# Function tables loaded ahead of use by one-column activations, and two norms that share one set of squares

## The reference

```python
h = h + _mixer(_rmsnorm(h, norm_mix_w), w_in, ...)      # retention and latent attention, gated
h = h + _swiglu(_rmsnorm(h, norm_ffn_w), ...)           # silu(u @ w_gate) * (u @ w_up) @ w_down
h = _rmsnorm(h, norm_final_w)[:, N_META:]               # end of block 1
...
for layer in range(2):                                  # block 2
    h = _rmsnorm_2(x, mix_norm_g[layer])                # layer 0: the second norm in a row
    x = x + (_even_mixer(h, ...) if layer == 0 else _odd_mixer(h, ...))
    x = x + square(relu(_rmsnorm_2(x, mlp_norm_g[layer]) @ w1)) @ w2

def _rmsnorm(xf, w):
    return xf * lax.rsqrt(jnp.mean(xf * xf, axis=-1, keepdims=True) + 1e-6) * w
```

## Time and profile before

| what | value |
|---|---|
| median of three runs | 1150.87 us (1149.94 to 1151.02) |
| the profiled execution, its time | 1150.63 us |
| span of its trace | 1148.5 us |
| PE busy | 1107.4 us (96%) |
| DVE busy | 732.2 us (64%) |
| ACT busy | 516.2 us (45%) |
| mean granted clock of PE | 0.982 of full |
| DMA | 177.64 MB, 155 GB/s |
| the chain that ended last | PE 79%, DVE 11%, ACT 6%, issue 2%, DMA 2% |

### The profile page before, as it was taken

One profiled execution on the slowest core, in us unless ns is written; L12 is line 12 of the kernel. 1 busy time (PEld: TensorE's weight loads), 2 busy tenths in 40 slices (PEclk: granted clock), 3 DMA queues, 4 the chain that ended last, 5 costly groups with the idle time before them and its releaser, 6 DMA issues.

```text
span 1148.5 us, 21011 instructions
## 1 busy us (share of the span) xinstructions
PE 1107.4 (96%) x8656; PEld 1058.8 (92%) x8656; DVE 732.2 (64%) x790; ACT 516.2 (45%) x521; POOL 2.2 (0%) x5
## 2 busy tenths in 40 slices
PE   8999999999999999989989999999988999999998
PEld 7998887899899999978879999999988999999998
DVE  5754646668666766667745665555589776655553
ACT  5523426444544444473755434342543464433431
POOL 0000000000000000000000000000000000000000
PEclk8999999999999999998989999999989999999999
DMA  9683242346456566726234455555244334655531
GB/s 307 188 219 111 74 129 74 111 148 189 140 153 202 169 197 181 235 94 220 74 111 147 146 191 175 194 171 170 88 144 145 116 114 146 216 184 183 182 110 37
DMA packets 162589, 177.64 MB, mean 155 GB/s; under 512 B 4800, under 2 KB 148288, under 8 KB 162536
## 3 DMA queue, kind: packets, MB, share of 16 engines
q1 hardware_dynamic: 160704, 174.58, 48.1%
q10 hardware_dynamic: 1832, 2.30, 1.1%
HBM read 175.29 MB, written 1.57 MB: 154 GB/s over the span
## 4 chain that ended last, share of the span: by engine, by line
PE 79%; DVE 11%; ACT 6%; issue 2%; DMA 2%; ACTq 0%; SPq 0%; DVEq 0%
PE proj L440 48%; PE aux L846 21%; DVE wlo L1525 4%; DVE f L1528 2%; DVE f L1525 2%; ACT whi L1108 2%; PE aux L497 1%; DMA gamma_rows<-f 1%; PE aux L608 1%; PE aux L597 1%; DVE f L1531 1%; ACT u L1308 1%; DMA f<-in_x_dram 1%; PE aux L720 1%; PE aux L705 0%
## 5 line engine op out<-in xcount | busy, mean ns | idle before, releaser
L440 PE MATMUL proj<-u,whi 128*128 128x256 f32 (+1 forms) x2912 | 537.8, 286 | 10.2 <-DVE wlo L1525 4.1
L440 PEld LDWEIGHTS proj<-u,whi 128*128 128x128 f32 x2912 | 455.6, 191 | 18.2 <-issue 7.4
L1525 DVE TENSOR_TENSOR wlo<-raw,whi 128x2048 fp32r<-128x2048 f32 (+2 forms) x179 | 374.7, 2093 | 149.1 <-ACT whi L1108 141.3
L440 PE MATMUL proj<-u,wlo 128*128 128x256 f32 (+1 forms) x1456 | 413.5, 284 | 0.0
L1108 ACT ACTIVATE whi<-raw 128x2048 fp32r<-128x2048 f32 (+2 forms) x173 | 309.5, 1789 | 105.4 <-PE aux L846 38.3
L440 PEld LDWEIGHTS proj<-u,wlo 128*128 128x128 f32 x1456 | 278.8, 191 | 0.0
L846 PE MATMUL aux<-v,whi 128*128 128x256 f32 x1376 | 249.9, 283 | 2.7 <-DVE v L1525 2.5
L846 PEld LDWEIGHTS aux<-v,whi 128*128 128x128 f32 x1376 | 214.1, 192 | 3.4 <-issue 3.4
L846 PE MATMUL aux<-v,wlo 128*128 128x256 f32 x688 | 194.6, 283 | 0.0
L846 PEld LDWEIGHTS aux<-v,wlo 128*128 128x128 f32 x688 | 131.8, 192 | 0.0
L440 PE MATMUL proj<-v,whi 128*128 128x256 f32 (+1 forms) x564 | 103.8, 286 | 1.8 <-DVE v L1528 1.2
(11 more groups left out here) (291 smaller groups left out, 750.9 us busy)
## 6 DMA issues: line engine op xcount, KB each, us to landing
raw<-in_mlp_w_dram SPq DMA_DIRECT2D x64, 1024.0 KB, 5.3
raw<-in_w_in_dram SPq DMA_DIRECT2D x21, 1024.0 KB, 6.8
raw<-in_od_w_in_dram SPq DMA_DIRECT2D x12, 1024.0 KB, 5.4
raw<-in_w_ffn_gate_dram SPq DMA_DIRECT2D x22, 512.0 KB, 4.0
raw<-in_w_ffn_up_dram SPq DMA_DIRECT2D x22, 512.0 KB, 5.2
raw<-in_w_ffn_down_dram SPq DMA_DIRECT2D x21, 512.0 KB, 5.3
raw<-in_ev_w_in_dram SPq DMA_DIRECT2D x10, 1024.0 KB, 5.3
raw<-in_w_ret_out_dram SPq DMA_DIRECT2D x4, 1024.0 KB, 5.3
```

Of the source, the lines that this page charges most:

```text
L440: ins = mm(o, w_of(a, k), x_of(b, k), start=first and k == 0 and j == 0, stop=last and k == kt - 1 and j == 2, skip_group_check=skip)
L1525: return ve.tensor_tensor(o, a, b, op)
```

## The change

There are two parts.

**Tables.** `table_for(func)` is an ACTIVATE of one column into a scratch column. The compiler puts the table load in front of it, and not in front of the next real use. It stands at some twenty places of ACT's program. One gelu (`za1`) is moved ahead of the second half's Exps. Both programs hold 25 ACT_TABLE_LOADs in all (the loops hold none).

**Norms.** With s = mean(x^2), the combined factor is 1/sqrt(mean(x^2 (g^2 + eps)) + eps^2), since mean((x g)^2)/(s + eps) + eps, times (s + eps), is just that sum. The weights of the sum of squares become g^2 + eps, broadcast (`gains_and_eps`), and one root gives the factor. The first norm's own sum is now a separate set of eight products of ones (`first_sums`) between `sq0` and `sq1`; its root and reciprocal, and the scaling of x, come later.

```diff
@@ PE
+    weights = gains_and_eps[:, k:k + 1].to_broadcast([P, P]) if second else C("ones")
+    ins = mm(aux[:, 0, 0:tokens], weights, sq_of(tokens)[:, k, :], start=k == 0, stop=k == KT - 1, ...)
-                if second and c:
-                    for k in range(0 if c == 1 else 2 * c, 2 * c + 2):
-                        ins = mm(aux[:, 1, 0:S], C("ones"), f("f3", 0, KT, S)[:, k, :], ...)
...
+            def first_sums():
+                for k in range(KT):
+                    ins = mm(aux[:, 1, 0:S], C("ones"), sq_of(S)[:, k, :], start=k == 0, stop=k == KT - 1)
+                ins.then_inc(sems["first_sums"], 1)
...
             project("sq0", t0=META, t=S, gate=by_pair(2, second=True))
-            for name in ("sq1", "sk0", "sk1"):
+            first_sums()
+            project("sq1", t0=META, t=S)
+            turn_norm(2)
+            for name in ("sk0", "sk1"):
                 project(name, t0=META, t=S)
-            turn_norm(2)
@@ ACT
+            def table_for(func):
+                A.run(act(small[:, 17:18], one, func))
...
             eng.wait_ge(sems["small_ready"], 1)
+            table_for(ACT.Sqrt)
...
+                        if c == 3:                       # norm("wo"), norm("eo"), norm("oo")
+                            table_for(ACT.Sqrt)
...
-                    if second:
-                        A.run(ins)
-                        for k in (2 * c, 2 * c + 1):
-                            ins = act(f("f3", 0, KT, S)[:, k, :], x2[:, k, :], ACT.Square, scale=V("final", k))
...
             norm("wo", lambda k: V("ffn", k), 1)
+            pump(loop_first["ffn"])
+            table_for(ACT.Tanh)
             hidden_layer(FFN)
-            norm(0, lambda k: both_gains[:, k:k + 1], 2, second=True)
-            eng.wait_ge(sems["second_mean"], 1)
-            A.post(act(r_all[:, 2, 0:S], r_all[:, 2, 0:S], ACT.Sqrt, bias=eps, scale=1.0 / D), "second_root")
+            table_for(ACT.Sqrt)
+            norm(0, lambda k: both_gains[:, k:k + 1], 2, eps_ap=eps_sq)
+            eng.wait_ge(sems["first_sums"], 1)
+            root(aux[:, 1, 0:S], r_all[:, 1, 0:S], 1.0 / D, eps, "first_root")
             for j, name in enumerate(("sq", "sk")):
                 pump(index[f"{name}0"])
...
             A.post(act(stat[:, 4:6], stat[:, 2:4], ACT.Sqrt, bias=eps, scale=1.0 / 512), "vg_root")
+            table_for(ACT.Exp)
             sb_exp_abs(0)
             sb_exp_abs(1)
             sb_log(0)
             sb_log(1)
+            table_for(ACT.Exp)
             pump(index["za1"])
             sb_attn(0)
             sb_attn(1)
             pump(index["sv0"])
+            table_for(ACT.Gelu_apprx_tanh)
+            read_out("za1")
+            A.post(act(za[:, :, 0:512], za[:, :, 0:512], ACT.Gelu_apprx_tanh), "gelu_ready")
+            table_for(ACT.Exp)
             sb_exp_abs(2)
             sb_exp_abs(3)
             sb_log(2)
             sb_log(3)
-            read_out("za1")
-            A.post(act(za[:, :, 0:512], za[:, :, 0:512], ACT.Gelu_apprx_tanh), "gelu_ready")
+            table_for(ACT.Exp)
             pump(index["sv1"])
...
             pump(index["gates"])
+            table_for(ACT.Exp)
...
             A.post(act(ab, ab, ACT.Ln, bias=one), "gates_log")
+            table_for(ACT.Tanh)
@@ DVE
-            eng.wait_ge(sems["root_ready"], 5)
-            B.run(ve.reciprocal(rf, rms))
-            B.run(tt(rm, rf, rf, ALU.mult))
-            B.post(tt(rm, rm, aux[:, 1, 0:S], ALU.mult), "second_mean")
-            eng.wait_ge(sems["second_root"], 1)
-            B.run(ve.reciprocal(rm, rm))
-            B.post(tt(rms, rf, rm, ALU.mult), "rms_ready")
+            norm_scale(2)
...
+            qk_raw(0, 0, urgent=True)
+            eng.wait_ge(sems["late_in"], 16)
+            B.run(ve.tensor_copy(f("f5", 0, 16, 64)[0:16], ...))
+            B.run(ve.tensor_copy(ident_r, C("ident")))
+            B.run(ts(mask_r, LC("mask_strict")[:, 0:P], 1.0, ALU.subtract, MASKED, ALU.mult))
+            qk_raw(0, 1)
+            eng.wait_ge(sems["first_root"], 1)
+            B.run(ve.reciprocal(rf, rf))
+            final_scale(0, 2)
+            qk_raw(1, 0)
+            token_factors(1)
+            final_scale(2, 6)
+            qk_raw(1, 1)
```

More of the change, by code:

```diff
@@ L280, in build @@
         both_gains = small[:, 64:72]
+        gains_and_eps, eps_sq = small[:, 8:16], small[:, 3:4]
         x_tok = f("f1", 0, 3, D)
@@ L1295, in _, with norm @@
             pump(index["mo1"])
-            def norm(source, gain, norm_no, second=False):
+            def norm(source, gain, norm_no, eps_ap=eps):
                 for c in range(4):
                     if isinstance(source, str):
+                        if c == 3:
+                            table_for(ACT.Sqrt)
                         pump(index[f"{source}{min(c + 1, 3)}"])
@@ L1321, in norm @@
                 eng.wait_ge(sems["sumsq"], norm_no + 1)
-                root(aux[:, 0, 0:S], r_all[:, 0, 0:S], 1.0 / D, eps, "root_ready")
+                root(aux[:, 0, 0:S], r_all[:, 0, 0:S], 1.0 / D, eps_ap, "root_ready")
             def hidden_layer(d):
@@ L1565, in _ @@
             B.run(ve.memset(eps, EPS))
+            B.run(ve.memset(eps_sq, EPS * EPS))
             B.run(ve.memset(gn_eps, GN_EPS))
@@ L1609, in _ @@
                      par[:, PAR_COLS["mix2"][0]:PAR_COLS["mix2"][0] + KT], ALU.mult))
+            final_gains = par[:, PAR_COLS["final"][0]:PAR_COLS["final"][0] + KT]
+            B.run(tt(gains_and_eps, final_gains, final_gains, ALU.mult))
+            B.run(ts(gains_and_eps, gains_and_eps, EPS, ALU.add))
             pump(index["rq0"] - AHEAD + 2)
@@ L1961, in _, with qk_raw, final_scale @@
             B.run(ts(qg8, V("sb_q"), 0.125, ALU.mult))
-            for j, name in enumerate(("sq", "sk")):
-                for c in range(2):
-                    b = arrive(f"{name}{c}", urgent=j == c == 0)
-                    freed(tt(pre[j][:, 2 * c:2 * c + 2, :], proj[:, b:b + 2, 0:S], bc(rms, 2), ALU.mult))
-                    if j == 0:
-                        for k in range(4 * c, 4 * c + 4):
-                            B.run(stt(x2[:, k, :], x2[:, k, :], V("final", k), rf, ALU.mult, ALU.mult))
+            def qk_raw(j, c, urgent=False):
+                b = arrive(f"{'sq' if j == 0 else 'sk'}{c}", urgent=urgent)
+                freed(tt(pre[j][:, 2 * c:2 * c + 2, :], proj[:, b:b + 2, 0:S], bc(rms, 2), ALU.mult))
+            def final_scale(k0, k1):
+                for k in range(k0, k1):
+                    B.run(stt(x2[:, k, :], x2[:, k, :], V("final", k), rf, ALU.mult, ALU.mult))
+            qk_raw(0, 0, urgent=True)
+            eng.wait_ge(sems["late_in"], 16)
+            B.run(ve.tensor_copy(f("f5", 0, 16, 64)[0:16], C("ident")[0:16, 0:16][:, :, None].to_broadcast([16, 16, 64])))
+            B.run(ve.tensor_copy(ident_r, C("ident")))
[8 more added lines that the diff above has]
+            qk_raw(1, 1)
             def per_token(name, dst, width=256):
```

15 lines of the change are left out of this document (4 added, 11 removed).

## The result

The changed kernel takes 1139.52 us in the median of its first four runs (1136.87 to 1140.48), the one before 1150.94. The ratio is 0.9898, with a 95% interval of 0.9884 to 0.9911, so 1.0% less. The forecast was 1138.3, in a range of 1134 to 1143. In a second group of six runs the same kernel took 1138.06 (1134.75 to 1141.11; 0.9895 of before, 0.9878 to 0.9913). The kernel before took 1149.1 to 1154.1 in all groups.

A forecast was written before the change was run, and what follows sets the result against it. PE was taken as the bound, busy 1107.4 of 1148.5 us, leaving only its gaps to win. The terms -1.3 - 1.5 - 1.0 - 0.5 + 0.2 - 8.3 = -12.4 took 1150.63 to 1138.2; forecast 1138.3, range 1134 to 1143.

The forecast's parts named there:

- The second norm, -8.3: Second norm: without PE's wait for a low half and the slower clock behind it, `za2` starts 8.3 us earlier.
- Rival A: Second norm: PE waits for the first sums instead, and the clock may fall again; 1139.3 to 1142 us, chance 0.12.
- the stated bound: Second norm: if PE never waits from 494.69 on, its 0.54 us wait goes too, giving -8.8.
- Start, -1.3: Start of the kernel: the Sqrt load moves to the very start, and 1.3 us of PE's 1.41 gap go.
- the feed-forward norm, -1.5: Norm ahead of the feed-forward loop: moved Sqrt and Tanh loads remove PE's gap of 1.54 us, giving -1.5.
- The attention, -1.0 and -0.5: Attention: first half, moved Exp load closes a 1.20 us gap but for 0.2; second half, moved gelu and loads give -0.5.
- The gates, +0.2: Gates: Exp load leaves PE's gap (1.28 us), but Tanh load delays a split DVE waits for (1.52); net +0.2.
- Rival C: Behind the gap of 5.5 us or the gates: a stretch of slow clock does not fall; 1135.5 us, chance 0.12.
- B: Second norm and where x is scaled: DVE's work gives 3 to 4 us back; 1142 us, chance 0.12.
- D: Loads ahead of weight splits, some twenty places: each costs 1.52 us, making the kernel slower, about 1152; chance 0.02.
- E: Table loads do not stay where put; only the second norm's gain remains; 1143 us, chance 0.02.
- the 0.02 for no change: Whole kernel: chance 0.02 of no change, for example the second norm's gain lost altogether by a late low half everywhere.

The follow-up runs named there:

- late_split3: The changed kernel with three squares of 256 columns, results unused, ahead of the split of `sk0` on ACT; 1138.15 us, beside the changed kernel's 1138.06.
- late_split6: The changed kernel with six squares of 256 columns, results unused, ahead of the split of `sk0` on ACT; 1142.42 us.
- tanh_late: The changed kernel with the Tanh load behind the gates' Log moved from ahead of two weight splits to behind them; 1137.96 us, 0.9886 of before.
- norms_only: The changed kernel with an empty `table_for` and the gelu of `za1` back behind the logs, so the norms alone; 1144.96 us, 0.9943 of before.

## Why the prediction was right

**The mechanism.** The argument was that only what reaches one of PE's gaps counts, and so it was: the sum of -12.4 meets 11.4 and 12.3 in the two groups of runs, and the gaps are gone where it said.

**The second norm, -8.3.** Measured 8.25, from `sq0` to `za2` (3.81 to 12.06), and 8.2 with the norms alone. Its parts mostly hold, one by luck: `sq1` was to end at 513.71, on before's time; moved by the 3.8 us of the earlier terms, it ended at 509.88, that is 513.69. The slack was to be 1.3 with the turning, and was 1.3; `late_split3` and `late_split6` are its test. Rival A had the right place and the right kind of price: `late_split6` is what it would look like.

One step was misread and cancelled. The 0.54 that PE waited for the second pair was to stay, "for the high halves come before any of the removed squares". But two of the removed squares, those of the first pair, stood ahead of the second pair's high halves:

```profile
494.62 1.05 ACT L1314 ACTIVATE f<-x_all,par 128x256 f32<-128x256 f32 x2
495.71 1.05 ACT L1308 ACTIVATE u<-x_all,small 128x256 fp32r<-128x256 f32 x2
```

With them this wait went, and by the stated bound the term would have been -8.8. It stayed at 8.25 because `sq0`, cut into pieces by the sums, takes 6.24 us of PE and not 5.68 (its pieces in the chain are 0.95, 0.83, 0.91 and 3.55). The "root of 0.51" is not removed from ACT either: the first norm still has its root, only off the path to `sq0`.

**Start, -1.3, and the feed-forward norm, -1.5.** After the first norm PE is 2.0 ahead at 74 us, of which 1.4 is the gap that went; the rest is older than the gap: the clock from 8 to 20 us was 0.72 on the mean, 0.57 before. The second gave 1.8, its gap of 1.54 and 0.2 in the loop behind. The start is also where the second profile of the changed kernel is ahead: 1.8 of its 2.1 us are there at `sq0`.

**The attention, -1.0 and -0.5.** Measured -1.8 to the turning of ya: the gap of 1.2 went whole, and the other went from 5.5 to 4.93, 0.57. Both are right within 0.2.

**The gates, +0.2.** Right, and for the stated reason. The gap shrank by 1.28, and from the turning of the gates to the rows 1.3 came back, so that place gained nothing. What came back is a wait of 2.8 in place of a slow clock: before, PE waited for nothing there, but its clock was 0.78 from 835.1 to 842.9, so that it reached the rows as they were ready. At full clock it waits 1.3 for them without the Tanh load (`tanh_late`, `norms_only`) and 2.8 with it. On the timeline of ACT the load stands in front of the split:

```profile
818.60 1.28 ACT L1126 ACT_TABLE_LOAD   x1
819.89 0.20 ACT L1126 ACTIVATE small<-small 128x1 f32<-128x1 f32 x1
820.13 3.87 ACT L1113 ACTIVATE whi<-raw 128x2048 fp32r<-128x2048 f32 x2
```

The dummy took 0.20 us, against the 0.24 with its pause that was taken, so this price was right too. In this kernel a moved load costs 1.5 us where it stands (818.60 to 820.13). The dummy starts 1.29 after the load's start, so nothing stands between them. The Trainium skill ("ScalarE: Activation LUTs", "What ACT_TABLE_LOAD costs") gives 1283 ns for the load and a drain of 1380 ns with it; the trace agrees with the first and contradicts the second.

**What was wrong: "Without a gap there, nothing is seen that would drop the clock."** It held around the second norm, but the sum took it for all that follows. In seven of the ten profiles with this order on PE the clock falls at about 541 us in or just behind the products with 16 rows, without any wait, and costs 3.1 us, in two of them 1.5. It was not to be seen in the profile of before, where the same products ran at full clock. Rival C had the clock give more; it also can take. Behind the gates it took 1.1 in both profiles of the changed kernel, a slow stretch longer than before's. In the two profiles of the changed kernel it did not fall there, and they are 1.3 and 3.5 us below the forecast for a profiled execution, 1138.2. If it fell in the other executions, as their clocks suggest, the median met the forecast in part by luck: losses of 3.1 and 1.1 stand against gains of 0.7 at the start, 0.2 at the feed-forward norm, and about 1 of slow clock behind the turning of ya (where the window has 0.69 for 0.54), and none of these was foreseen.

**The rivals.** A is refuted by the slack. B: DVE was busy for 19.27 of 22 us from 505 to 527 and PE waited for nothing there, so DVE kept up. D: loads ahead of splits cost something at one place, the gates. E: all loads that a dummy was to bring stand at the dummies (L1126); five others stand where no dummy was written, three of them at a Log. C, a stretch of slow clock less, is what the second profile shows at the start and behind ya; its 1134.75 is the fastest of its group, and the medians are not there.

**The chances.** Those of the forecast and the rivals A to E add up to 1.00, not to 0.98 as the text says, so the 0.02 for no change is one too many.

## What to carry to other kernels

Look for the gap that PE waits in last, and ask for each instruction in front of its release whether PE needs it now: a weight preparation that is two chunks early is the cheapest thing to move, and was worth 7 to 9 us here, as much as the removed work. A gap on PE can have two prices, its length and the slow clock behind it (here 2.5 or 1.6 us behind 4.1, 1.6 behind 2.0, none behind 0.4, and once none behind 2.8). A function-table load is worth moving only if it stands in such a chain, and the place it goes to must not be ahead of something that is waited for.

## What the runs showed of the hardware

A load of function tables took 1.28 us and a one-column activation behind it 0.20, with 0.01 to 0.02 between (818.60, 819.89). Weights of one column, broadcast, cost at most 0.05 us a sum: four sums with them took 1.92 us at the end of `sq0`, eight with plain ones 3.45, so 0.48 and 0.43 each. The clock of PE fell to its lower level while PE was fully busy, in five profiles in products of 16 rows and in two just behind them, and not in three others that do the same there. One kernel's executions spread over 6 us (1134.75 to 1141.11) with mean clocks of 0.988 to 0.983, so that a change under 0.2% is seen here in the trace's places, not in the median.
